# Turning three of the four merged mixer tiles by DVE block transposes and 16 GpSimd transfers each

## What is computed

```python
h = rms_norm(x, mix_pre_gain[l])
proj = h @ w_in[l]
# y_a: stick-breaking attention, y_b: spatial gating, y_c: S5 state space
y_a = attention_out @ w_br_a[l]      # K = 1024
y_b = gating_out @ w_br_b[l]         # K = 512
y_c = s5_out @ w_br_c[l]             # K = 512
g = sigmoid(gates).reshape(b, s, 3, d)
merged = g[:, :, 0] * y_a + g[:, :, 1] * y_b + g[:, :, 2] * y_c
x = x + rms_norm(merged @ w_out[l], mix_post_gain[l])
# then cross-attention into 256 memory tokens, and
gt, up = jnp.split(h @ w_ffn_in[l], 2, axis=-1)
x = x + rms_norm((jax.nn.silu(gt) * up) @ w_ffn_out[l], ffn_post_gain[l])
```

## Time and profile before

| | |
|---|---|
| median of 3 runs | 1534.1 us |
| profiled execution | 1534.13 us |
| its span | 1532.5 us |
| PE busy | 1511.5 us (99%) |
| DVE busy | 924.6 us (60%) |
| ACT busy | 770.9 us (50%) |
| GpSimd (POOL) busy | 122.9 us (8%) |
| mean DMA rate | 198 GB/s |
| mean granted TensorE clock | 0.995 |

### The profile page before, as it was taken

One profiled execution on the slowest core, in us unless ns is written; L12 is line 12 of the kernel. 1 busy time (PEld: TensorE's weight loads), 2 busy tenths in 40 slices (PEclk: granted clock), 3 DMA queues, 4 the chain that ended last, 5 costly groups with the idle time before them and its releaser, 6 DMA issues.

```text
span 1532.5 us, 20260 instructions
## 1 busy us (share of the span) xinstructions
PE 1511.5 (99%) x6846; PEld 1245.6 (81%) x6846; DVE 924.6 (60%) x1105; ACT 770.9 (50%) x934; POOL 122.9 (8%) x225
## 2 busy tenths in 40 slices
PE   9999999999999999999989999999999999999996
PEld 6887887888888888888868888888888888888885
DVE  7778998754554677557565555555555555444444
ACT  7645445665566444666556444444444444444342
POOL 0000000000000000000000222220122222000001
PEclk9999999999999999999999999999999999999999
DMA  9655555555555656755435666665666666555553
GB/s 336 232 183 180 177 185 182 194 177 169 180 174 170 233 192 226 285 196 199 164 125 176 209 205 206 206 204 198 204 207 207 209 201 234 198 192 193 193 193 108
DMA packets 87739, 302.68 MB, mean 198 GB/s; under 512 B 11984, under 2 KB 12240, under 8 KB 86672
## 3 DMA queue, kind: packets, MB, share of 16 engines
q1 hardware_dynamic: 80096, 285.12, 55.7%
q0 software_dynamic: 7168, 16.53, 3.1%
q10 hardware_dynamic: 432, 0.45, 0.1%
HBM read 294.19 MB, written 2.10 MB: 193 GB/s over the span
## 4 chain that ended last, share of the span: by engine, by line
PE 98%; DVE 1%; DMA 0%; ACT 0%; SPq 0%; issue 0%; DVEq 0%; ACTq 0%
PE acc L1328 18%; PE acc L1330 18%; PE acc L1329 18%; PE side L1328 11%; PE side L1330 11%; PE side L1329 11%; PE tr L1328 3%; PE tr L1330 3%; PE tr L1329 3%; PE tr L1345 1%; DMA raw<-in_units 0%; DVE xres L1309 0%; PE side L1384 0%; PE tr L1391 0%; PE side L1409 0%; PE side L1440 0%
## 5 line engine op out<-in xcount | busy, mean ns | idle before, releaser
L787 DVE TENSOR_TENSOR w_lo<-raw,w_hi 128x1024 fp32r<-128x1024 f32 x531 | 649.8, 1225 | 552.2 <-ACT w_hi L434 547.3
L434 ACT ACTIVATE w_hi<-raw 128x1024 fp32r<-128x1024 f32 x531 | 562.2, 1060 | 665.5 <-PE acc L1330 356.4
L1328 PE MATMUL acc<-w_hi,xT_hi 128*128 128x512 f32 x860 | 338.2, 393 | 1.6 <-DVE w_lo L787 1.6
L1329 PE MATMUL acc<-w_lo,xT_hi 128*128 128x512 f32 x860 | 335.4, 390 | 0.0
L1330 PE MATMUL acc<-w_hi,xT_lo 128*128 128x512 f32 x860 | 335.4, 390 | 0.0
L1328 PEld LDWEIGHTS acc<-w_hi,xT_hi 128*128 128x128 f32 x860 | 161.9, 188 | 37.4 <-issue 3.5
L1330 PEld LDWEIGHTS acc<-w_hi,xT_lo 128*128 128x128 f32 x860 | 161.9, 188 | 34.0
L1329 PEld LDWEIGHTS acc<-w_lo,xT_hi 128*128 128x128 f32 x860 | 162.0, 188 | 32.9
L1328 PE MATMUL side<-w_hi,xT_hi 128*128 128x512 f32 x480 | 187.0, 390 | 0.0
L1329 PE MATMUL side<-w_lo,xT_hi 128*128 128x512 f32 x480 | 186.8, 389 | 0.0
L1330 PE MATMUL side<-w_hi,xT_lo 128*128 128x512 f32 x480 | 186.8, 389 | 0.0
(11 more groups left out here) (325 smaller groups left out, 1556.0 us busy)
## 6 DMA issues: line engine op xcount, KB each, us to landing
raw<-in_units SPq DMA_DIRECT2D x531, 512.0 KB, 3.3
hT_st<-h_blk POOLq DMA_DIRECT2D x176, 32.0 KB, 2.8
x_tok<-in_x SPq DMA_DIRECT2D x4, 512.0 KB, 5.8
xres<-in_x POOLq DMA_DIRECT2D x1, 2048.0 KB, 10.6
m_raw<-in_mem_t POOLq DMA_DIRECT2D x1, 2048.0 KB, 8.6
mq<-in_mem POOLq DMA_DIRECT2D x1, 2048.0 KB, 15.4
x_raw<-in_x_t SPq DMA_DIRECT2D x7, 256.0 KB, 6.4
out<-xres SPq DMA_DIRECT2D x3, 512.0 KB, 2.8
```

The source lines that it names most:

```text
L434: a_.activation(w_hi[:, j % RING], raw[:, j % RING], ACT.Copy).then_inc(hi_ready, 1)
L787: v_.tensor_tensor(w_lo[:, s], raw[:, s], w_hi[:, s].bitcast(F32), ALU.subtract).then_inc(lo_ready, 1)
L1328: pe.matmul(bank(b, h), hi[:, kt, tok], w_hi[:, s, k], start=begin, stop=False)
L1329: pe.matmul(bank(b, h), hi[:, kt, tok], w_lo[:, s, k], start=False, stop=False)
```

## The change

Tiles 0, 1 and 2 of `merged` (turned in the loop, groups 1 to 3) no longer go through PE. DVE transposes 32x32 blocks of `mg` into a new buffer `m_blk`, GpSimd moves them in 16 transfers into `m_st`, ACT rounds into `xT_hi`, DVE subtracts into `xT_lo`. The code of the FFN is made into shared helpers for that. The fourth tile is still turned by PE in `U_OUT`. The counter base of PE's turns moves from 10 to 4 (`T_X1`), since six turns are gone.

```diff
+        m_blk = at("m_blk", 112, [HALVES, 4, 4, 32])
+        m_st = at("m_st", 116, [HALVES, 4, 4, 32])
...
 GpSimd
+            def spread(dst, src, done):
+                for a in range(4):
+                    for b in range(4):
+                        g.dma_start(dst[32 * a:32 * a + 32, :, b].rearrange("p h k c -> p h (k c)"),
+                                    src[32 * b:32 * b + 32, :, a].rearrange("p h k c -> p h (k c)")).then_inc(done, 16)
+
+            for i in range(1, 4):
+                pool.wait_ge(m_blocked, i)
+                if i > 1:
+                    pool.wait_ge(m_lo, i - 1)
+                spread(m_st, m_blk, m_turned)
             pool.wait_ge(mg_ready, 4)
...
 ScalarE (ACT)
+            def blocks_hi(dst, src, k0, landed, count, done):
+
+                act.wait_ge(landed, count)
+                a_.activation(dst[:, bass.ds(k0, 4)].rearrange("p k (g c) -> p k g c", c=32),
+                              src[:].rearrange("p h b k c -> p k (h b) c"), ACT.Copy).then_inc(done, 1)
...
-                    if j == 1 and before:
-                        turn_hi_parts(i * 2 + (T_BR - 2), xT_hi, i * 4 - 4)
+                    if j == 6 and before:
+                        blocks_hi(xT_hi, m_st, i * 4 - 4, m_turned, i * 256, m_hi)
...
 VectorE (DVE)
+            def to_blocks(dst, src, done):
+
+                for h in range(HALVES):
+                    last = v_.transpose(dst[:, h].rearrange("p a k c -> p k a c"),
+                                        src[:, h].rearrange("p (k a c) -> p k a c", k=4, a=4))
+                last.then_inc(done, 1)
+
+            def blocks_lo(dst_hi, dst, src, k0, hi_done, count, done):
+
+                dve.wait_ge(hi_done, count)
+                ks = bass.ds(k0, 4)
+                v_.tensor_tensor(dst[:, ks].rearrange("p k (g c) -> p k g c", c=32),
+                                 src[:].rearrange("p h b k c -> p k (h b) c"),
+                                 dst_hi[:, ks].rearrange("p k (g c) -> p k g c", c=32).bitcast(F32),
+                                 ALU.subtract).then_inc(done, 1)
...
-                    if j == 1 and before:
-                        turn_lo_parts(i * 2 + (T_BR - 2), xT_hi, xT_lo, i * 4 - 4)
+                    if j == 0 and before:
+                        to_blocks(m_blk, mg, m_blocked)
+                    if j == 7 and before:
+                        blocks_lo(xT_hi, xT_lo, m_st, i * 4 - 4, m_hi, i, m_lo)
...
                         br = (j - 3) // 2
+                        if j == 3 and before:
+                            dve.wait_ge(m_blocked, i)
...
 TensorE (PE)
-                    if j == 1 and before:
-                        pe.wait_ge(mg_ready, i)
-                        turn(i * 2 + (T_BR - 2), mg[:])
...
                 if n == 0:
-                    pe.wait_ge(turn_lo, T_BR + 6)
+                    pe.wait_ge(m_lo, 3)
```

More of the change, by code:

```diff
@@ L61 @@
     0, 1, 4, 12, 13, 15, 23, 35, 39, 40, 41, 42, 46, 68)
-T_GLU, T_BR, T_X1, T_X2 = 0, 2, 10, 18
+T_GLU, T_BR, T_X1, T_X2 = 0, 2, 4, 12
 N_X, N_GM, N_Y1, N_MEM, N_X1, N_Y2, N_X2, N_Y3 = range(8)
@@ L266, in trunk @@
             sem("mq_squared"))
+        m_blocked, m_turned, m_hi, m_lo = sem("m_blocked"), sem("m_turned"), sem("m_hi"), sem("m_lo")
         h_blocked = sem("h_blocked")
@@ L400, in spread_blocks @@
                     pool.wait_ge(hT_ready, i - 1)
[L401 to L404, removed]
+                spread(hT_st, h_blk, hT_turned)
             spread_blocks(1)
@@ L476, in turn_hi_parts @@
                     last.then_inc(turn_hi, 1)
+            def blocks_hi(dst, src, k0, landed, count, done):
+                act.wait_ge(landed, count)
+                a_.activation(dst[:, bass.ds(k0, 4)].rearrange("p k (g c) -> p k g c", c=32),
+                              src[:].rearrange("p h b k c -> p k (h b) c"), ACT.Copy).then_inc(done, 1)
             def hidden_hi(i):
[L480 to L483, removed]
+                blocks_hi(hT_hi, hT_st, i * 4 - 4, hT_turned, i * 256, hT_hi_ready)
             def root(n, k):
@@ L652, in _ @@
                     if n == 0 and j == 2:
-                        turn_hi_parts(T_BR + 6, xT_hi, 12)
+                        turn_hi_parts(T_BR, xT_hi, 12)
                     if j == 4:
@@ L814, in hidden_turn @@
                     dve.wait_ge(acc_taken[h], i * 2 + G_FI)
[L815 to L818, removed]
+                to_blocks(h_blk, hb, h_blocked)
             def hidden_lo(i):
[L822 to L827, removed]
+                blocks_lo(hT_hi, hT_lo, hT_st, i * 4 - 4, hT_hi_ready, i, hT_ready)
             def inverse(n, width, squares):
@@ L1188, in _ @@
                     if n == 0 and j == 2:
-                        turn_lo_parts(T_BR + 6, xT_hi, xT_lo, 12)
+                        turn_lo_parts(T_BR, xT_hi, xT_lo, 12)
                     if j == 4:
@@ L1475, in out_step @@
                         pe.wait_ge(mg_ready, 4)
-                        turn(T_BR + 6, mg[:])
+                        turn(T_BR, mg[:])
                 if n == 0:
-                    pe.wait_ge(turn_lo, T_BR + 6)
+                    pe.wait_ge(m_lo, 3)
                 chunk(U_OUT, CU * n, n + G_OUT, 6, xT_hi, xT_lo, out_step, last=False, b=n % 2, lag=2)
                 if n == 0:
-                    pe.wait_ge(turn_lo, T_BR + 8)
+                    pe.wait_ge(turn_lo, T_BR + 2)
                 chunk(U_OUT, CU * n + 6, n + G_OUT, 2, xT_hi, xT_lo, first=False, k0=6 * UK, b=n % 2)
```

## The result

The changed kernel takes 1538.5 us (median of 11 runs, 1535.5 to 1539.2), the kernel before 1534.1 us (median of 11, 1533.4 to 1536.5). The ratio is 1.0022, with a 95% interval from 1.0014 to 1.0030: slower by 0.22%. The ratio goes by all the runs and is smaller than that of the medians, which lie 4.4 us (0.29%) apart. I had forecast 1532.8 us and a range up to 1535.8. The profiled execution of the changed kernel is one of 1538.53 us, with a span of 1536.9 us where it was 1532.5.

A forecast was written before the change was run, and what follows sets the result against it. PE was taken to bound the kernel: 1534.13 - 2.61 (three turns removed) + 1.1 (new wait at U_OUT) + 0.2 (late tile) = 1532.8 us. The range was 1530.0 to 1535.8 us.

The forecast's parts named there:

- The bound: Whole kernel: PE, busy 1511.5 of 1532.5 us and 98% of the chain, so only what PE executes or waits for counts.
- the price of a turn: Eight transposes of mg on PE between units 1 and 2 of a group: 0.87 us.
- the number of turns: Three turns (24 of 32 transposes) leave PE in the loop, taking off 2.61 us.
- The new wait: Start of U_OUT: PE waits once for DVE's subtraction of the third tile, losing 1.1 us with the restart.
- DVE's order as its floor: End of loop: the tile's subtraction follows step 6's weight subtraction on DVE, ending 0.78 us after PE is ready.
- The clock fall before the FFN: Rival, PE's residual wait: low clock there gone, 1530.3 us, chance 0.15; or longer, up to 1533.7, chance 0.06.
- a difference below 3.1 us can't be told from none: Whole kernel: a difference under about 0.2% can't be distinguished by measurement, even the whole saving of 2.61 us.
- Does the tile arrive in time?: Third tile's transfers, landing in 3.6 us, delay ACT's step 6 rounding by 0.2 us; bounds nothing to 0.6.
- pass 2 hidden: Passes 1 and 2 of the loop: the ring hides the tile's lateness, as step 6's unit is needed 8.2 us later.
- T0: The end of a group's last unit, from which the forecast counts the turned tile's DVE work, transfers and landing.
- Transfers late: Rival: POOL or DMA held up between block transposes and step 6; 1537.7 us if POOL stood still; chance 0.09.
- The new wait brings a low clock: Rival at the start of U_OUT: clock falls at PE's wait, costing 2.5 to 3.2 us, about 1535.6; chance 0.04.

The follow-up runs named there:

- experiment 2: Changed kernel with only the first half of each weight unit loaded for units 172 to 207 (256 KB loads); 1532.65 us in one run.
- experiment 7: Changed kernel with the transfers of tiles 2 and 3 moving only the first token half, 16 KB instead of 32 KB; 1532.59 us in one run.
- experiment 4: Changed kernel, PE's third-tile wait before unit 4 of U_OUT, the turned tile's ACT rounding and DVE subtraction at step 7; 1531.56 us, ratio to before 0.9977.
- experiment 1: Changed kernel with PE's wait for the third tile moved from before unit 0 to before unit 4 of U_OUT; 1536.6 us, ratio to before 1.0013.
- experiment 5: experiment 4 with DVE's weight subtractions of steps 3, 5 and 7 ahead of the gate work; 1536.9 us, ratio 1.0013.
- experiment 6: Kernel before the change with one wait added on PE at the start of U_OUT, until DVE has prepared its unit 3; 1540.88 us, ratio 1.0043.
- experiment 3: Changed kernel with four f32 matmuls added on PE between the loop and the wait for m_lo; 1537.0 us, ratio to before 1.0017.
- experiment 8: experiment 4 with DVE's block transposes at step 2 instead of step 0 of the next group; 1531.9 us, ratio 0.9983.

## Why the prediction was wrong

**Right.** The bound, the price of a turn and the number of turns: the loop ends 2.51 us earlier for a forecast of 2.61. The new wait, its place, its being met once, and DVE's order as its floor: where the transfers landed in time (experiments 2 and 7), PE waited 0.8 us and the time was 1532.65 and 1532.59 us, against a forecast of 1532.8. The two times are of one run each and could be nearer by chance; the wait of 0.8 us is what the traces show. Eight transposes of `mg` are left, and POOL's pace is that of the FFN. The clock fall before the FFN did not go away. Wrong was the remark that a difference below 3.1 us can't be told from none: the intervals here are 1.4 us wide to either side, and that of experiment 4, 2.7 us faster, excludes 1.

**The step that failed** is "Does the tile arrive in time?", the term of 0.2 us. I took the landing of 3.6 us from the FFN and its upper bound, 4.0, from the same place. It was 5.6 to 5.8 us for the third tile, and PE waited 4.0 us where 0.8 and the 0.2 were forecast. Two things of the sum were off. The transfers started 0.9 us later than I had them, because ACT was already held up by the second tile's transfers, DVE by ACT, and the third tile's block transposes by DVE: they began at 581.66, and the last transfer's issue at 591.21 was 15.5 us after PE ended the group (575.7), not 14.6. I had called pass 2 hidden because the ring covered PE; the ring did cover PE, but the next tile's turn is in the same queue. And the landing took 2 us more. Together 2.9 us late, passed on one to one to PE.

**The cause of the 2 us** I had in my hands. I had worked out that DVE's weight subtractions of steps 7 and 0 would come late, at T0 + 3.8 and after, and priced this at nothing because PE had 3.2 us in hand. But each late subtraction also releases a load: SP's loads come in a burst that starts with the transfers, at 1.0, 2.1, 3.3 and 5.8 us behind the first transfer of the third tile, where the FFN's tile has three, at 1.4, 4.1 and 6.8. I had compared mean DMA shares, 0.59 for the stage against 0.75 beside the FFN's transfers, and taken the lower mean as an argument against late transfers. A mean over a group of 22 us says nothing on the 9 us in question: there the share was

```profile
583.25:591.75 8.50, 8.50 (x39) 7.06 (x38) 6.85 (x8) 3.18 (x3) 8.50 (x16) 1.00 0.88 278
591.75:597.50 5.75, 5.68 (x26) 4.37 (x24) 3.78 (x5) 1.60 (x2) 0.00 (x0) 1.00 0.98 226
```

in the changed kernel, 0.88 and then 0.98.

**The rivals.** "Transfers late" was the right one in place and sign, given 0.09; its mechanism, POOL standing still, was not: each issue took POOL 0.54 us, as in the FFN. "The new wait brings a low clock", given 0.04, came with it. I had treated them as separate and added no case with both. They are not independent: the clock held for the wait of 0.8 us in experiments 2 and 7, and fell with those of 3.0 us (experiment 1), 3.1 us (experiment 5) and 4.0 us (here, 2.6 us more). That is why the result lies 5.7 us above the forecast where the lateness alone would have made it about 3.

**What stays open.** How large the low clock's part in the medians is: the traces price it at 2.6 us in the changed kernel and 1.6 in experiment 6, and the median of experiment 3 is lower by 1.5 us, within the spread. Why a landing takes 5.0 us beside four loads in one group and 5.9 in another is not shown. Experiments 4 and 8 don't differ in time, so a late landing costs nothing once nobody stands behind it.

## What to carry to other kernels

A transfer between partitions that replaces TensorE work is only as good as the slack behind its landing; put its first reader at the latest step at which it can stand, and look at everything queued behind that reader on its engine, the source of the next tile included. When a change makes an engine late that frees load buffers, expect its loads in a burst, and count the loads that start beside the new transfers. The DMA share tells it only in the stretch in which the last of the transfers are in flight (0.97 to 1.01 where they were late, 0.82 or less where they were not). Over the whole 8 us of issue it does not: it was 0.91 for tile 1 of the changed kernel, which landed in 4.0 us, and 0.75 for tile 3 of experiment 4, which took 5.7. And give a wait on TensorE as long as those of 3.0 to 4.0 us here the price of the low clock behind it, not its length alone.

## What the runs showed of the hardware

A hole of 4.0 us in PE's work, with nothing else changed, cost 6.9 us in the median, 5.8 of them in its own stage by the trace. Transfers of 32 KB within SBUF landed in 4.1 us at most in this stage with three 512 KB loads started during their issue, in 4.8 to 5.9 us with four, and in 6.2 to 6.4 us with five. With four loads of half the size it was 2.9 us, and with transfers of half the size beside four full loads 4.0. Each issue took POOL 0.50 to 0.54 us in all of these, so its pace is no sign of how late the data will be.
